# Attention in parity classes of tokens for two dilated groups; early normalisation and a turned gate for two other groups, in a fused transformer kernel

## The reference

```python
# branch a: 8 heads over all keys (256 tokens are one block); branch b: 3 x 8 heads, dilated
for gi, (w, d) in enumerate(((128, 1), (512, 4), (2048, 16))):
    # query t sees the keys t - steps, steps = 0, d, 2d, ... <= w
    lse = logsumexp(logits); outs += [exp(logits - lse) @ v]; lses += [lse]
o_b = sum(softmax(lses)[gi] * outs[gi])
# branch c: window of 128 keys, with a sink in the denominator
m = max(max(logits), sink); e = exp(logits - m); p = e / (sum(e) + exp(sink - m))
branches = [o_a * silu(ga), o_b * silu(gb), o_c * silu(gc)]
merged = sum(sigmoid(gate_i) * (branches[i] @ w_branch[i]))
x = x + merged @ w_out
```

## Time and profile before

| | us |
|---|---|
| median of 3 runs | 991.71 (991.48 to 991.83) |
| the profiled execution | 991.65 |
| its span, first to last instruction | 989.80 |

### The profile page before, as it was taken

One profiled execution on the slowest core, in us unless ns is written; L12 is line 12 of the kernel. 1 busy time (PEld: TensorE's weight loads), 2 busy tenths in 40 slices (PEclk: granted clock), 3 DMA queues, 4 the chain that ended last, 5 costly groups with the idle time before them and its releaser, 6 DMA issues.

```text
span 989.8 us, 13394 instructions
## 1 busy us (share of the span) xinstructions
PE 983.2 (99%) x4952; PEld 794.7 (80%) x4952; DVE 629.4 (64%) x784; ACT 595.3 (60%) x930; POOL 12.2 (1%) x22
## 2 busy tenths in 40 slices
PE   8999999999999999999999999999999999999998
PEld 7888788888888777788888888877777777788887
DVE  5776776455556765675555465867667567777644
ACT  6776665454546655565454545766767668857561
POOL 1000000000000000000000000000000000000000
PEclk9999999999999999999999999999999999999999
DMA  8545266756563633457757654655443343436551
GB/s 283 175 126 196 85 204 200 235 175 205 170 212 127 211 131 128 142 179 241 229 193 226 227 186 141 211 170 181 149 137 127 108 147 128 130 126 213 195 187 43
DMA packets 106073, 170.26 MB, mean 172 GB/s; under 512 B 4020, under 2 KB 65334, under 8 KB 106032
## 3 DMA queue, kind: packets, MB, share of 16 engines
q1 hardware_dynamic: 103392, 161.23, 49.7%
q0 software_dynamic: 2304, 8.37, 2.6%
q10 hardware_dynamic: 336, 0.10, 0.0%
HBM read 168.58 MB, written 1.11 MB: 171 GB/s over the span
## 4 chain that ended last, share of the span: by engine, by line
PE 96%; DVE 2%; ACT 1%; DMA 1%; issue 0%; SPq 0%; DVEq 0%; ACTq 0%
PE acc L441 14%; PE acc L443 13%; PE acc L442 13%; PE acc L499 12%; PE pair_ps L443 7%; PE pair_ps L441 7%; PE pair_ps L442 7%; PE acc L736 3%; PE acc L558 3%; PE turn_ps L625 3%; PE acc L646 2%; PE pair_ps L613 2%; PE pair_ps L612 2%; PE turn_ps L517 1%; PE acc L593 1%; PE turn_ps L441 1%
## 5 line engine op out<-in xcount | busy, mean ns | idle before, releaser
L1698 DVE TENSOR_TENSOR w_lo<-w_raw,w_hi 128x2048 fp32r<-128x2048 f32 (+3 forms) x154 | 343.1, 2231 | 119.2 <-ACT w_hi L1056 118.5
L1056 ACT ACTIVATE w_hi<-w_raw 128x2048 fp32r<-128x2048 f32 (+3 forms) x154 | 286.4, 1863 | 74.8 <-PE acc L443 28.1
L441 PE MATMUL acc<-w_hi,uT_hi 128*128 128x512 f32 (+3 forms) x552 | 218.8, 396 | 1.0 <-DVE w_lo L2132 1.0
L443 PE MATMUL acc<-w_hi,uT_lo 128*128 128x512 f32 (+3 forms) x552 | 211.7, 384 | 0.0
L442 PE MATMUL acc<-w_lo,uT_hi 128*128 128x512 f32 (+3 forms) x552 | 211.1, 382 | 0.0
L441 PE MATMUL pair_ps<-w_hi,uT_hi 128*128 128x512 f32 x320 | 126.5, 395 | 0.0
L441 PEld LDWEIGHTS acc<-w_hi,uT_hi 128*128 128x128 f32 x552 | 103.7, 188 | 26.6 <-issue 7.0
L443 PE MATMUL pair_ps<-w_hi,uT_lo 128*128 128x512 f32 x320 | 124.8, 390 | 0.0
L442 PE MATMUL pair_ps<-w_lo,uT_hi 128*128 128x512 f32 x320 | 124.6, 389 | 0.0
L443 PEld LDWEIGHTS acc<-w_hi,uT_lo 128*128 128x128 f32 x552 | 103.6, 188 | 20.8
L442 PEld LDWEIGHTS acc<-w_lo,uT_hi 128*128 128x128 f32 x552 | 103.9, 188 | 17.7
(11 more groups left out here) (236 smaller groups left out, 1245.1 us busy)
## 6 DMA issues: line engine op xcount, KB each, us to landing
w_raw<-in_w_in SPq DMA_DIRECT2D x46, 1024.0 KB
w_raw<-in_w_gate SPq DMA_DIRECT2D x44, 512.0 KB
w_raw<-in_w_up SPq DMA_DIRECT2D x44, 512.0 KB
w_raw<-in_w_down SPq DMA_DIRECT2D x22, 1024.0 KB
w_raw<-in_w_out SPq DMA_DIRECT2D x12, 1024.0 KB
w_raw<-in_w_qkv SPq DMA_DIRECT2D x16, 512.0 KB
w_raw<-in_w_branch SPq DMA_DIRECT2D x6, 1024.0 KB
bias<-rel_rows POOLq DMA_DIRECT2D x5, 1024.0 KB, 7.5
```

What stands on the lines that cost most here:

```text
L441: mm(o, xh, wh[:, k, :], start=first and k == 0, stop=False)
L443: done = mm(o, xl, wh[:, k, :], start=False, stop=last and k == len(kts) - 1)
L1056: activation(w_hi[:, slot, 0:width], w_raw[:, slot, 0:width], ACT.Copy).then_inc(hi_done, 1)
L1698: v.tensor_tensor(w_lo[:, slot, 0:width], w_raw[:, slot, 0:width], w_hi[:, slot, 0:width].bitcast(f32), ALU.subtract).then_inc(lo_done, 1)
```

## The change

1. Groups 2 and 3 ("classes"): q, k and v are projected with the even tokens as block 0 and the odd ones as block 1. The activations' columns are read at a stride of two (`columns`), while the group before attends. Each head then has two 128x128 parts of logits instead of three; turns, exponentials, copies and values shrink with them. ACT writes the outputs back in token order (`by_class`), and scales with `class_scale`, per-token factors that POOL sends through DRAM into class order. Maxima and sums of these groups come back to token order through DRAM too (`class_stats`, `stats`). The tables of 128 columns come from a thinned copy of the rows.
2. Group 0 ("whole") and the window ("sink"): DVE normalises the probabilities ahead of their turn. The outputs stay turned: `turn_outputs`, DVE's token copies and the later scaling go, ACT copies into `turned_branch`. For the window the sink enters the maxima and sums pair by pair.
3. For these two branches PE turns the gate instead of the branch (`turn_swish`), DVE multiplies the turned branch by it and ACT rounds the result (`split_gated`). For group 0 this happens at step 4 of the window group, no longer at step 5.
4. The loop over groups 0 to 2 is written out on PE, ACT and DVE.

On PE:

```diff
+            def columns(x, kt, blk):
+
+                return x[:, kt, blk:S:TB] if n.classes else x[:, kt, tokens(blk)]
...
-                    xh, xl = x_hi[:, kt, tokens(blk)], x_lo[:, kt, tokens(blk)]
+                    xh, xl = columns(x_hi, kt, blk), columns(x_lo, kt, blk)
...
-                    done = mm(pair_ps[:, j, 128:384], q[:, 128:256], k, start=True, stop=True)
+                    if kind == "classes":
+                        done = mm(pair_ps[:, j, 128:256], q[:, 128:256], k[:, 128:256], start=True, stop=True)
+                    else:
+                        done = mm(pair_ps[:, j, 128:384], q[:, 128:256], k, start=True, stop=True)
...
-                if kind == "mla" or kind == "band":
+                if kind in ("mla", "band", "whole"):
                     pe.wait_ge(normed, pair0 + (t + 1) - 4)
+                elif kind == "sink":
+                    pe.wait_ge(normed, pair0 + (t + 1) - 16)
                 else:
                     pe.wait_ge(prob_done, pair0 + (t + 1))
...
-                    for i in range(3):
+                    for i in range(prob_width(kind) // P):
...
-                if kind != "last":
+                if kind in ("sb", "mla", "band"):
                     since(pe, out_read, pair0 + t if bank is out_ps else pair0 + t - 1)
+                else:
+                    since(pe, out_copied, pair0 + t - 16)
...
+                        if kind == "classes":
+                            done = mm(bank[HD * j:HD * j + HD, P * blk:P * blk + P], v,
+                                      prT[:, t % 2, j, P * blk:P * blk + P], start=True, stop=True, skip_group_check=True)
+                            continue
...
+                            if s == 4 and blk == 1 and closing:
+                                closing()
                             if s == 5 and blk == 1:
-                                if closing:
-                                    closing()
                                 attention_step(kind, 5, pair0, turn0)
-                                turn_outputs(2, pair0, turn0, outs)
+                                if not normed_first(kind):
+                                    turn_outputs(2, pair0, turn0, outs)
...
-                        if s in (3, 4):
+                        if s in (3, 4) and not normed_first(kind):
                             turn_outputs(s - 3, pair0, turn0, outs)
...
-            def turn_branch(i, banks):
+            for g in range(3):
+                project_and_attend((512, 512, 512), ("whole", "last", "classes")[g], g * 2 + 3, g * 6 + 36,
+                                   classes=g > 0)
+            project_and_attend((512, 512, 256), "classes", 9, 54)
...
+            def turn_swish(i, banks):
+                pe.wait_ge(swish_done, i + 1)
+                turn(lambda k, blk: swish[:, i, blk, P * k:P * k + P], 4, banks)
+
+            def turn_first_swish():
                 pe.wait_ge(logit_read, n.pair + 4)
-                turn_branch(0, pair_banks)
+                turn_swish(0, pair_banks)
...
-            project_and_attend((512, 512, 512), "last", 11, 60, window_outs, turn_full)
+            project_and_attend((512, 512, 512), "sink", 11, 60, closing=turn_first_swish)
...
-                if i:
-                    turn_branch(i, turn_banks)
+                if i == 1:
+                    turn_dilated()
+                if i == 2:
+                    turn_swish(2, turn_banks)
```

On ACT:

```diff
+                if kind == "sink":
+                    top = top8[:, :, 2 * t:2 * t + 2]
+                    activation(top, top, ACT.Exp)
...
-                    activation(outs[t % 2], out_ps[:, 0:S], ACT.Copy).then_inc(out_copied, 1)
-
-                if kind == "last":
+                    dst, src = outs[t % 2], out_ps[:, 0:S]
+                    if kind == "classes":
+                        dst, src = by_class(dst), src.rearrange("p (c i) -> p c i", c=TB)
+                    if normed_first(kind):
+                        dst = turned_branch(0 if kind == "whole" else 2, t)
+                    activation(dst, src, ACT.Copy).then_inc(out_copied, 1)
...
-            project_and_attend([swish_gate(1), swish_gate(2), lambda: gate_exponentials(0)], "last", 32, 8, outs=window_outs,
-                               after={3: factors(0, 1, 4), 5: lambda: split_banks(oT_hi, 0, 4, pair_banks)}, late=(2,))
+            def split_gated(i):
+                for k0 in (0, 2):
+                    act.wait_ge(swish_gated, n.gates + 1)
+                    activation(oT_hi[:, k0:k0 + 2, :].rearrange("p k t -> p (k t)"), branch_half(i, k0), ACT.Copy)\
+                        .then_inc(turned_hi, 1)
+                    n.gates += 1
+                    n.bank = n.bank + 1
+
+            n.gates = 0
+            project_and_attend([swish_gate(1), swish_gate(2), lambda: gate_exponentials(0)], "sink", 32, 8,
+                               after={3: dilation_factors, 4: lambda: split_gated(0)}, late=(2, 4))
...
-                if i:
-                    split_banks(oT_hi, 4 * (i % 2), 4, turn_banks)
+                if i == 1:
+                    split_banks(oT_hi, 4, 4, turn_banks)
+                if i == 2:
+                    split_gated(2)
```

On DVE:

```diff
+                if kind == "sink":
+                    link(done)
+                    lowest, top = [x[:, :, 2 * t:2 * t + 2] for x in (negmax8, top8)]
+                    sinks = sink[:, 2 * t:2 * t + 2].unsqueeze(1).broadcast_to([P, TB, 2])
+                    link(v.scalar_tensor_tensor(lowest, sinks, -1.0, lowest, ALU.mult, ALU.min))
+                    done = v.tensor_tensor(top, sinks, lowest, ALU.add)
                 done.then_inc(max_done, 1)
+
+            def class_maxima(t, pr, pair0, bias_of):
+
+                for blk in range(TB):
+                    cols = block_cols("classes", blk)
+                    done = v.scalar_tensor_tensor(pr[:, :, blk, ::-1], pair_ps[:, :, cols][:, :, ::-1], HD ** -0.5,
+                                                  bias_of(t), ALU.mult, ALU.add)
+                done.then_inc(logit_read, 1)
+                dve.wait_ge(logit_read, pair0 + (t + 1))
+                v.tensor_reduce(negmax8[:, :, 2 * t:2 * t + 2].rearrange("p b j -> p j b"), pr, op=ALU.max, axis=AX.X,
+                                negate=True).then_inc(max_done, 1)
...
+                if kind == "sink":
+                    sums, top = [x[:, :, 2 * t:2 * t + 2] for x in (total8, top8)]
+                    link(v.tensor_tensor(sums, sums, top, ALU.add))
...
+                    if normed_first(kind) and 1 <= s < 5:
+                        normalise(kind, s - 1, n.pair)
                     attention_step(kind, s, n.pair, head0, bias_of)
-                    if 3 <= s:
+                    if 3 <= s and not normed_first(kind):
                         token_outputs(s - 3, n.pair, head0)
...
+                dve.wait_ge(rel_ready, 1)
+                v.tensor_copy(thin, rel_f[:, P - 1:REL:2]).then_inc(thinned, 1)
...
+            def dilation_maxima():
+                dve.wait_ge(stat_full, 32)
...
+            def split_gated(i, banks, copied):
+
+                dve.wait_ge(out_copied, copied)
+                for k0 in (0, 2):
+                    dve.wait_ge(turned, n.bank + k0 // 2 + 1)
+                    o = branch_half(i, k0)
+                    v.tensor_tensor(o, o, banks[k0 // 2], ALU.mult).then_inc(swish_gated, 1)
+                for k0 in (0, 2):
+                    dve.wait_ge(turned_hi, n.bank + 1)
+                    lo, hi = [t[:, k0:k0 + 2, :].rearrange("p k t -> p (k t)") for t in (oT_lo, oT_hi)]
+                    v.tensor_tensor(lo, branch_half(i, k0), hi.bitcast(f32), ALU.subtract).then_inc(turned_lo, 1)
+                    n.bank = n.bank + 1
 
...
-            project_and_attend(6, "last", 32, table(0), {
-                0: full_over_total, 1: lambda: swish_gate(1), 2: first_gate, 3: lambda: swish_gate(2),
-                4: dilation_weights}, closing={5: lambda: split_banks(oT_hi, oT_lo, 0, 4, pair_banks)}, late=(2,))
+            project_and_attend(6, "sink", 32, table(0), {
+                1: lambda: swish_gate(1), 2: dilation_maxima, 3: lambda: swish_gate(2), 4: dilation_weights},
+                closing={4: lambda: split_gated(0, pair_banks, 4)}, late=(2, 4))
...
-                if i:
-                    split_banks(oT_hi, oT_lo, 4 * (i % 2), 4, turn_banks)
+                if i == 1:
+                    split_banks(oT_hi, oT_lo, 4, 4, turn_banks)
+                if i == 2:
+                    split_gated(2, turn_banks, 20)
```

More of the change, by code:

```diff
@@ L241, in build_program, with by_class, block_cols, normed_first @@
         stored = sem("stored")
+        def by_class(x):
+            return x.rearrange("p (i c) -> p c i", c=TB)
+        def block_cols(kind, blk):
+            return slice(P * blk, P * blk + P) if kind == "classes" else key_cols(blk)[0]
+        def normed_first(kind):
+            return kind in ("whole", "sink")
```

(28 more changed lines are left out.)

151 lines of the change are left out of this document (92 added, 59 removed).

## The result

| | before, us | changed, us |
|---|---|---|
| median | 991.65 (991.48 to 991.83) | 1000.31 (999.52 to 1002.46) |
| the profiled execution | 991.65 | 999.52 |
| its span | 989.80 | 997.8 |
| mean granted clock of the executions | 1.000 | 0.997, 0.995, 0.997, 0.997 |

The changed kernel is slower: ratio 1.0091, 95% interval 1.0077 to 1.0104, so +8.7 us where +3.7 was forecast. It also spreads by 3 us, where before spreads by 0.4.

The account below looks back on a forecast made before the run. PE, busy for 99% of the span, was taken as the bound: 9.65 us of new waits less 6.0 saved gives +3.7, so 991.65 + 3.7 = 995.3 us; range 990.5 to 1000.0, likeliest case 992.8 to 996.7.

Parts of the forecast that it names:

- Savings by classes: Groups 2 and 3, PE: narrower logits, fewer turns, narrower values save 0.62 us per pair, 5.0 in all, 4.6 kept.
- No turn of outputs: Group 0 and window, PE: eight turns of outputs go, 1.4 us saved.
- Waits 1: Group 0, steps 2 and 4: PE's probability turn waits for DVE's normalisation behind the head norm, 2.25 and 2.4 us.
- Wait 2: Window, step 3: PE's turn waits for DVE's normalisation behind w_lo, 1.5 us.
- Wait 3: Window, steps 4 and 5: PE's last values wait for the gate's chain in ACT's queue, 3.5 us.
- Rivals 3 and 4: Rival 3: wait 3 hidden, 991.8, 0.15; rival 4: normalising ahead of PE's turn, 989.2, 0.08; without wait 3, 985.7, 0.04.
- Weights at a stride: Projections of groups 2 and 3: 288 strided weight loads stay hidden, 0 us; +6 at twice the load length.
- rival 2: Clock falls at the window's 3.5 us standstill; 3 to 6 us at the lower clock give 997 to 998.5; chance 0.10.
- Covered, at nothing: Branch stage's extra DVE multiplies (1.2 us if uncovered), statistics through DRAM, small DMAs and thinning copy at start: 0 us.

Follow-up runs that it names:

- plain columns: Changed kernel with projections of groups 2 and 3 reading activations' columns side by side, not at a stride of two (wrong tokens): median 997.12 us, profiled execution 997.95.
- k4: Changed kernel with three edits of DVE's order: normalisation earlier in group 0 (steps 2, 4) and window (step 3), gate multiplies earlier: median 987.95 us, ratio to before 0.9964.
- the kernel with the early gate: Changed kernel with DVE's two multiplies by the turned gate moved ahead of pair 3's probability copy and weights' subtraction, window step 4: median 994.64 us.

## Why the prediction was wrong, point by point

- **Savings by classes, 5.0, with 4.6 kept**: right. With plain columns group 2 is 2.63 us shorter and group 3 2.12, or 2.59 with the 0.47 of new waits at its end put back: 0.65 per pair where 0.62 was summed. These 0.5 were put at 0.4. Group 3's last turn waits 0.60 for ACT behind the gate work, and 0.14 comes with the next group's keys.
- **No turn of outputs, 1.4**: 1.2, but only as the rest of the ledger. With the standstills taken out (`k4`, and `k4` without parity) 0.6 to 0.7 shows, and 0.2 is taken by a wait that stays; where the remaining 0.3 to 0.4 goes is open.
- **Waits 1, 2.25 and 2.4**: 2.04 and 2.18. **Wait 2, 1.5**: 1.31. **Wait 3, 3.5**: 3.37. All four at the named place, behind the named operation, each 0.1 to 0.2 too long by my sum. (In wait 3 the named terms give T + 4.41 for PE and not T + 4.45, which changes nothing.) Rivals 3 and 4 are out: no wait was hidden.
- **Weights at a stride, 0 (0 to +6)**: 1.4. One failed step is "a load up to 1.8 times as long is hidden: 0". I took the spacing of narrow matmuls as the length that a load may have, and so treated it as all or nothing; the rows show that a load 7 ns longer lengthens the pace by 5 ns, with 40 ns of apparent room. The Trainium skill, "SBUF — State Buffer", row on cachelines in the section "Specifications (TRN2)", led to 0 as well: two accesses in a line for full bandwidth. The measured loads are 4% longer (195 against 188 ns), so here its rule holds only nearly.
- **The clock falls, 0.10 in rival 2, and only at the 3.5 us standstill**: this is the step that failed most. It is worth 3.4 us in the median execution and 5 in the slowest. I gave it a small chance because the clock was 1.000 over the span, but that row speaks of a PE that never stood over 1.1 us; for the four standstills that I forecast it says nothing. And I let only the longest count, where 2.00 us suffices. Its price as I worked it out for 3 to 6 us of the lower clock, 1.5 to 3, was right (1.7).
- **Covered, at nothing** (branch stage, statistics, start): right, no row of PE waits there.

Without a fall the changed kernel would take 996.1 (the profiled 999.52 less 3.4) to 996.6 us (from `k4`), against 995.3 forecast: the 1.4 for the loads, less some tenths from waits that were shorter. The rest of the miss, about 4 us to the median, is the clock's. The range ended at 1000.0, and rival 2, bounded at one fall, at 998.5; the profiled execution has two falls, and by time and clock none of nine executions has fewer.

## What to carry to other kernels

An operation that moves onto a queue in order costs the place where it stands, not its length: 1.2 us of scaling behind the wrong neighbour cost up to 2.2 us, and three edits of DVE's order, nothing else, turned +8.7 us into -3.7. When a wait of about 2 us or more is forecast for a PE that was never idle, add the clock's price to it as a likely term (here 1.7 us each, in most executions with such a wait), not as a rival. Price the two halves of a change apart before keeping both: here the parity classes bring 3.3 us, and the early normalisation with the turned gate some 0.6, against 12.4 us of standstills and falls that came with them.

## What the runs showed of the hardware

- One standstill of 2.00 us of a PE otherwise busy was followed by 3.4 us at 1.2 GHz in 9 of 11 executions, one of 2.60 in 7 of 11, one of 1.41 in none of 11. In the ten falls of the profiles the lower clock began between 0.3 us before PE went on and 1.5 us after. It cost 1.7 us whatever the standstill's length, 2.00 to 3.41 us. In the changed kernel the 2.18 us wait had no fall in two profiles, and had one in the profile of the kernel with the early gate. What decides between the two is open.
- Weight loads that read fp32 at a stride of two take 195 ns in place of 188, and each adds 5 ns to a chain of 512-wide matmuls.
- An ACT copy from PSUM reading 256 columns at a stride of two takes no longer (0.46 to 0.50 us) than one that reads them side by side.
